# Value sums behind a group's first stage: order of work on PE in a hybrid decoder step

## What is computed

```python
q = (x @ w_query).reshape(t, PEER_HEADS, 2, PEER_DK // 2)
s = jnp.einsum('thcd,ckd->thck', q, sub_keys)
sv, si = lax.top_k(s, PEER_TOPK)
cand = sv[:, :, 0, :, None] + sv[:, :, 1, None, :]      # 16 x 16 sums, top 16 again
top_s, pos = lax.top_k(cand, PEER_TOPK)
g = jax.nn.softmax(top_s, axis=-1)
u = expert_u[experts]
v = expert_v[experts]
a = jax.nn.gelu(jnp.einsum('td,thkd->thk', x, u))
return jnp.einsum('thk,thkd->td', g * a, v)
```

## Time and profile before

| | |
|---|---|
| median of 3 runs | 3510.18 us (3496.6 to 3515.45) |
| profiled execution | 3510.76 us, span 3509.0 us |
| PE busy | 2510.7 us, 72% |
| VectorE busy | 2278.5 us, 65% |
| GpSimd busy | 2300.2 us, 66% |
| ScalarE busy | 813.6 us, 23% |
| value sums on PE (L924) | 4096 matmuls, 1176.0 us |
| u and v gathers | 2048, 1082.26 MB by the software queue |
| all DMA | 1279.45 MB, mean 365 GB/s |
| mean granted clock of PE | 0.839 of full speed |

### The profile page before, as it was taken

How to read it: one execution, slowest core, us unless ns; L and a number is a source line. 1 busy time by engine, 2 the same in 40 slices (tenths; PEclk the granted TensorE clock), 3 DMA queues, 4 the chain that set the end, 5 groups by cost and what they waited for, 6 DMA issues and landing times.

```text
span 3509.0 us, 38717 instructions
## 1 busy us (share of the span) xinstructions
PE 2510.7 (72%) x11488; PEld 1386.8 (40%) x11488; DVE 2278.5 (65%) x5454; ACT 813.6 (23%) x2057; POOL 2300.2 (66%) x2068
## 2 busy tenths in 40 slices
PE   7558775878764598877644977778546888875755
PEld 6426443545531264445311643345213534332421
DVE  3685586655688756657898466558796454544874
ACT  2112212232212212322112123322113122222111
POOL 0466575755657777676777767667777585657774
PEclk9779887999986799898876999889777798988776
DMA  6699899988999999999999999899999999999997
GB/s 237 241 389 375 329 410 333 392 306 302 372 346 373 373 402 372 353 369 412 408 359 375 405 385 355 329 376 409 400 368 374 379 388 359 371 334 398 411 409 305
DMA packets 368935, 1279.45 MB, mean 365 GB/s; under 512 B 59372, under 2 KB 77974, under 8 KB 353368
## 3 DMA queue, kind: packets, MB, share of 16 engines
q0 software_dynamic: 297216, 1082.26, 80.6%
q1 hardware_dynamic: 62324, 168.67, 12.5%
q10 hardware_dynamic: 9188, 26.05, 2.3%
HBM read 1262.31 MB, written 13.48 MB: 364 GB/s over the span
## 4 chain that ended last, share of the span: by engine, by line
DVE 37%; PE 31%; DMA 15%; issue 7%; ACT 4%; SPq 3%; POOL 2%; DVEq 0%; ACTq 0%; POOLq 0%
DVE u_ring L1736 15%; PE acc L924 9%; DMA u_ring<-in_expert_u,pick_cur 8%; PE front L586 8%; PE front L802 3%; DMA v_ring<-in_expert_v,pick_cur 3%; DVE si_u L1603 2%; SPq L536 2%; DVE sv L1602 2%; PE front L711 2%; DMA w_ukT<-in_cache_krope 2%; DVE work L1603 2%; DVE work L1602 1%; DVE work L1647 1%; DVE work L1649 1%
## 5 line engine op out<-in xcount | busy, mean ns | idle before, releaser
L924 PE MATMUL acc<-v_ring,diag 128*64 128x512 f32 x4096 | 1176.0, 723 | 614.6 <-ACT diag L1222 344.4
L1851 POOL DMA_INDIRECT v_ring<-in_expert_v,pick_cur x1024 | 1146.5, 1120 | 607.3 <-PE acc L924 334.3
L1851 POOL DMA_INDIRECT u_ring<-in_expert_u,pick_cur x1024 | 1136.9, 1110 | 569.1 <-issue 292.3
L1736 DVE CUSTOM_DVE_ANT_0 u_ring<-u_ring,xn_cur 128x1024 f32<-128x1024 f32 x1024 | 1209.9, 1222 | 335.1 <-DMA u_ring<-in_expert_u,pick_cur 329.4
L924 PEld LDWEIGHTS acc<-v_ring,diag 128*64 128x64 f32 x4096 | 342.6, 164 | 1331.4 <-issue 878.5
L1222 ACT ACTIVATE diag<-ident,wgt 128x64 f32<-128x64 f32 x1024 | 272.8, 338 | 787.1 <-DVE wgt L1742 734.9
L586 PE MATMUL front<-work,w_ring 128*128 128x256 f32 (+2 forms) x1536 | 306.4, 341 | 31.8 <-DVE mo L1337 17.1
L586 PE MATMUL front<-mo,w_ring 128*128 128x256 f32 (+2 forms) x1536 | 298.2, 335 | 0.0
L1215 ACT ACTIVATE gelu<-dots 128x4 f32<-128x4 f32 x256 | 52.7, 206 | 996.5 <-DVE dots L1736 992.8
L586 PEld LDWEIGHTS front<-work,w_ring 128*128 128x128 f32 x1536 | 249.0, 199 | 83.9 <-issue 28.6
L586 PEld LDWEIGHTS front<-mo,w_ring 128*128 128x128 f32 x1536 | 252.0, 198 | 23.9
(11 more groups left out here) (303 smaller groups left out, 2375.7 us busy)
## 6 DMA issues: line engine op xcount, KB each, us to landing
w_ring<-in_w_pieces SPq DMA_DIRECT2D x112, 1024.0 KB, 8.4
u_ring<-in_expert_u,pick_cur POOLq DMA_INDIRECT x1024, 10.5
v_ring<-in_expert_v,pick_cur POOLq DMA_INDIRECT x1024, 9.9
x_t<-in_x_prompt SPq DMA_DIRECT2D x16, 512.0 KB
v_ring<-in_w_pieces SPq DMA_DIRECT2D x8, 1024.0 KB, 12.0
work<-in_cache_ckv SPq DMA_DIRECT2D x64, 128.0 KB, 15.2
xn_cur<-scratch ACTq DMA_DIRECT2D x14, 512.0 KB, 9.7
scratch_x<-rows_next ACTq DMA_DIRECT2D x8, 512.0 KB, 6.8
```

The lines of the kernel that those rows point to most:

```text
L924: last = nc.tensor.matmul(acc[rows, half, :], diag[:, s % RING, :], v_ring[:, s % RING, half * 512:half * 512 + 512], start=(s < 2), stop= ...
L1736: v.tensor_tensor_reduce(u_ring[:, slot, :], u_ring[:, slot, :], xn2_cur[:, block_of(r), :], 1.0, 0.0, ALU.mult, ALU.add, dots[:, g * G + ...
L1851: pool.indirect_dma_start(ring[:, slot, :], None, a[table][0], bass.IndirectOffsetOnAxis(ap=pick, axis=0)).then_inc(loaded[slot], 16)
```

## The change

PE does the value sums of a group behind its first stage in all groups, not only in those with pages. Which stages a group has, and the order on all other engines, stay.

```diff
@@ -985,11 +985,10 @@
             def tile(it):
 
                 for g, stages in enumerate(PLAN[it]):
-                    ahead = 1 if has_pages(stages) else len(stages)
-                    for s in stages[:ahead]:
+                    for s in stages[:1]:
                         stage(*s)
                     v_group(it, g)
-                    for s in stages[ahead:]:
+                    for s in stages[1:]:
                         stage(*s)
 
             def turn_weights():
```

## The result

The changed kernel takes 3538.84 us (median of 6 runs, 3536.64 to 3541.12) beside 3504.52 us for the kernel before (6 runs): ratio 1.0092, 95% interval 1.0077 to 1.0107. It is slower by 27 to 38 us. The forecast was 3511 us; the time lies in the range, and it is the slower rival's (3547 us) that it is near to. It lies outside the 3493 to 3528 us that the prediction gave its own case.

A forecast was written before the change was run, and what follows sets the result against it. The prediction took tile 1 as paced by the PE, ScalarE, VectorE ping-pong, and GpSimd and DMA as bounding where VectorE awaits u gathers. Costs 41.6 - 16 - 25 = +0.6 us on 3510.76 gave 3511 us; range 3470 to 3550.

The forecast's parts named there:

- the slower rival: Value sums stand ahead of work VectorE needs, full price, no gain from GpSimd: +37 us, 3547 us; chance 0.28.
- The bound of tile 1: From 584 to 912 us the ping-pong of PE, ScalarE and VectorE sets the pace; GpSimd is ahead of need.
- Heads, 8 x 2.55 = 20.4 us: In eight head groups, value sums before the next transpose delay it by 2.55 us each: a cost of 20.4 us.
- Output projection: Value sums ahead of the projection's last piece, which VectorE awaits: 3.6 us in tile 1, 5 at the sample.
- Attention output to mix norm, 5 x 1.7: In five groups, value sums between attention output and the norm's matmul end 1.7 us late: cost 8.6 us.
- the 5.6 us of the query projections: Value sums outlast the 1.16 us gap ahead of the scores: 0.7 us charged in each of eight groups.
- the 5.0 of the query pairs: Two pairs of query stages, charged 2.5 us each for value sums moved between their stages.
- Input projections in tile 4, 2.6 us: Value sums wait for late v gathers, so the projection starts late: net cost 2.6 us.
- Hand-overs, 16 us: At five hand-overs, value sums no longer precede the next group's first stage: gain of 2.5 to 3.6 us each.
- GpSimd's earlier release, 25 us: Earlier value sums let GpSimd issue later gathers sooner, cutting VectorE's u waits: 25 us gained, 0.7 of 35.
- Value sums wait longer for their gathers: PE's wait for v gathers, 269.9 us before, should rise; no size given.
- No effect: DMA is the bound, so costs and gains both vanish: 3511 us; chance 0.16.

The follow-up runs named there:

- Tile 1 alone: Kernel before with value sums moved behind the first stage only in the second tile's groups (19 of the 67): 3644.65 us, ratio 1.0089.
- heads-alone kernel: Kernel before with value sums moved only in the 8 groups that begin with a head and have more than one stage: 3635.77 us, ratio 1.0077.
- the kernel with the value sums inside the stage: Kernel before with value sums put behind the scores, ahead of the value matmuls, in 26 groups whose last stage is a head: 3620.59 us, 1.0015.
- The kernel with the hand-overs alone: Kernel before with value sums moved only in the 15 groups whose first stage is a norm or turn of rows: 3615.75 us, ratio 1.0001.
- All but the heads: Kernel before with value sums moved behind the first stage in all groups but those that hold a head: 3612.13 us, ratio 1.0000.
- the late release: Changed kernel where a v gather also waits until PE has issued the last stage of two groups before: 3669.27 us, 1.0067 against the kernel before.
- the second set: Later runs on the chip numbered 5, with the changed kernel again against the kernel before: 3657.48 us, ratio 1.0039.

## Why the prediction was right or wrong

That 3538.84 us lies between 3470 and 3550 is no merit of the sum. The range took in both rivals; the forecast, no change to speak of, missed by 28 us and had its sign from two sides that cancel, and the prediction gave "slower by over 0.5%" 0.31. What follows takes its terms one by one.

**The bound of tile 1: right.** The prediction had the ping-pong of PE, ScalarE and VectorE set the pace there and GpSimd ahead of need. In the stretch of tile 1 both GpSimd's wait for PE (68.9 to 46.7 us) and VectorE's for u gathers (18.4 to 4.9) got shorter, and it took 19 us longer. Tile 1 alone makes the kernel 0.89% slower.

**Heads, 8 x 2.55 = 20.4 us: right in mechanism, and near in size with some luck.** The transpose of the pattern came 2.5 us behind the scaled probabilities (737.01 to 739.49), as drawn. The eight groups 15, 16, 40, 41, 44, 45, 46 and 88 changed by +0.2, +4.3, +2.4, +3.9, -4.9, +3.4, +3.8 and +2.3 us: 15.4 together, 20.3 without group 44. The single values don't carry the term evenly: groups 16 and 46 have an attention output and no transpose behind the value sums, which the prediction read as the same case; in 44 the transposes became ready only when the value sums were done; 88 is anywhere from 17.4 to 28.8 us in kernels that don't move it; and about 3.6 us of the growth in tile 1 is PE's lower clock, on which the prediction put no price. The heads-alone kernel puts the eight at 28 us (17 to 39 by its interval). The prediction named PE's delay as the price; the place where it counts is VectorE's copy, as the kernel with the value sums inside the stage showed.

**Output projection: right in tile 1, not seen at the sample.** Group 50 grew from 35.28 to 38.82 us, 3.5 where 3.6 was charged. The 5 us of the sample tokens' end aren't there: groups 229 to 235 take 84.5 us before and 84.1 after.

**Attention output to mix norm, 5 x 1.7: not seen.** Group 42 got 1.5 us shorter. The value sums at 761.98 end where the norm's matmul starts (765.56), but VectorE's squares ended at 764.50, so about 1 us is late and the next weight isn't. With all such moves and no heads the time stays at 1.0000, so none of these smaller terms can be told from zero, nor can the 5.6 us of the query projections and the 5.0 of the query pairs.

**Input projections in tile 4, 2.6 us: not seen.** Groups 132 to 136 take 61.5 us before and 60.9 after. The 4.5 us lost in this tile's first part come in group 142 (22.38 to 26.62), where the prediction had nothing; why there, the runs don't tell.

**Hand-overs, 16 us: seen in single places, not in the sum.** The query piece follows the row transposes directly, and starts 0.13 us behind the group's weight where it was 3.39 us: these are the 3.3 us predicted. (The prediction's last paragraph names value sums straight behind the row transposes as the sign; that is the order of before, its own reckoning puts them ahead.)

```profile
916.93 1.97 PE L593 MATMUL front<-ident,rows_next 128*128 128x128 f32 x8 [5.57 <-DVE rows_next L1587]
920.27 3.78 PE L586 MATMUL front<-work,w_ring 128*128 128x256 f32 x8 [1.38 <-DVE mo L1594]
```

Yet group 52 grew from 20.33 to 21.73 us. The eight matmuls of 920.27 take 3.78 us where those of 905.65 took 1.99, at a granted clock of 0.50 for 1.00: before, the value sums ran between PE's idle time and them. And the group's own value sums, 3.65 us, now stand ahead of its key scores. Group 44 did win 4.9 us: its first scores no longer stand behind the value sums of group 43. The largest hand-over was one that the prediction didn't price, and it shows how such a gain is lost. Group 31, before:

```profile
602.58 1.89 PE L586 MATMUL front<-mo,w_ring 128*128 128x256 f32 x8
604.40 3.65 PE L924 MATMUL acc<-v_ring,diag 128*64 128x512 f32 x16
604.50 28.61 SPq L484 DMA_DIRECT2D w_ring<-in_w_pieces  x4
608.19 1.42 DVE L1749 TENSOR_TENSOR y_t<-acc,y_t 128x512 f32<-128x512 f32 x2 [8.45 <-PE acc L924]
```

and after:

```profile
600.77 4.81 PE L924 MATMUL acc<-v_ring,diag 128*64 128x512 f32 x16
606.66 1.41 DVE L1748 TENSOR_TENSOR y_t<-acc,y_t 128x512 f32<-128x512 f32 x2
612.71 25.17 SPq L484 DMA_DIRECT2D w_ring<-in_w_pieces  x4
632.15 0.96 DVE L1356 TENSOR_TENSOR work<-work 128x768 f32<-128x768 f32 x1 [9.47 <-ACT x_t L1092]
```

VectorE waited 8.45 us before for the finished sums of tile 0; with the value sums ahead of the projection piece this wait is gone, and the group is 8.5 us shorter (22.76 to 14.22). But the piece itself ends late, the weight load that waits for it starts 8.2 us later (604.50 to 612.71), and two groups on VectorE waits 9.47 us for the projection: group 33 grows from 6.88 to 16.69 us. PE ran from 605.51 us to this projection without a gap, so it isn't the load that VectorE waited for: the order on PE only chose who waits. The kernel with the hand-overs alone has the same pair (group 31 14.23 us, group 33 14.76) and a ratio of 1.0001.

**GpSimd's earlier release, 25 us: this step failed.** The prediction took 0.7 of 35 us. All but the heads makes nearly all of these moves; by the prediction's own terms it should have stood near 52.6 - 20.4 - 11 - 16 - 25 = -20 us, a ratio of 0.9945, and it was 1.0000 (from 0.9967). With its costs taken as charged, that speaks against the two gains together; what speaks against this one is the waits, and the late release, in which 25 us should have been lost. The u gathers did come earlier: VectorE's wait of 5.62 us in tile 0 is 2.21 us in its place, and over the span its u waits fell by 22.5 us, inside the 20 to 40 that were named. But this was no time won. GpSimd's wait for dot products rose by 133.4 us as its wait for PE fell by 109.4, which the prediction had written down as the sign that the lead is worthless. Nor was there a gain where it was placed, in us from weight to weight: groups 9 to 20, 181.5 to 190.0 (8 predicted); 193 to 200, at the sample's projections, 111.2 to 112.7 (12.5 predicted). The error was in taking a shorter wait of VectorE for u gathers as time won. The ring holds two groups, and GpSimd can't be further ahead of VectorE than that; it got there sooner and stood there. Whether a smaller part of the 25 us exists stays open: the late release cost 12 us beside the change, with nothing to some 20 us by its noise.

**Value sums wait longer for their gathers: right in sign.** PE's wait rose from 269.9 to 319.6 us, and to landing a v gather now takes a median of 11.8 us after 9.9:

```profile
v_ring<-in_expert_v,pick_cur POOLq DMA_INDIRECT x1024, 11.8
```

The granted clock, on which the prediction put no price, stayed at 0.839 in the mean over the span, while it fell in single places (0.50 at 750 us).

**The rivals.** "No effect" was ruled out by the ratio, and with it DMA as the one bound of the whole: tile 1 moves 336 GB/s and the later slices up to 412. The slower rival said "full price and no gain from GpSimd", 37 us; 28 (between the profiled executions) to 34 us (between the medians) were measured first and 12 (3657.48 less 3645.9) in the second set. Its 37 is near partly by luck: it is 52.6 less 16, while the heads alone cost 28 us, and all the rest, the costs outside the heads, the hand-overs and GpSimd's lead, comes to nothing within 12 us together. The forecast was the other case only because two gains of 41 us together were credited from single places. Stretches without a moved group kept their pace, as they had to: groups 70 to 73 took 44.2 us in both kernels and 181 to 191 took 135.3 and 135.2, which are the two that the prediction named. The limit of about 358 GB/s that the prediction took from the Trainium skill ("DMA: Bandwidth & Descriptors", section "Bandwidth") would have left the change without effect. After as before there are slices at 411 and 412 GB/s, and the measurement decides. The section doesn't disagree as much as the prediction has it: it gives the 358 for two cores that stream at once and up to 425 GB/s for one core alone.

## What to carry to other kernels

When work is moved ahead in an engine's queue, ask which engine reads the result that now stands behind it, and whether that reader has anything else to do: 3.65 us of value sums ahead of a 0.55 us transpose cost VectorE 2.4 to 3.9 us in a group, and behind the same transpose and its scores, ahead of the values, no cost was seen (1.0015, 0.9987 to 1.0043). A producer that is released earlier gains only if its ring isn't full when it gets there; look for the wait that will replace the one removed, and credit nothing until the consumer's own wait is shown to be on the path. Work that filled an engine's idle time may also have kept its clock up: look at the lengths of the same matmuls before and after. Try the few places with a clear price apart from the many without: 8 of 67 groups held the price.

## What the runs showed of the hardware

Halving the columns of the value sums took PE's mean granted clock from 0.826 in the changed kernel of that set to 0.737 and 0.738 in the two halved ones. Their time fell by only 1.0 to 1.5%. Other matmuls got longer: those of the projections on L586 took a mean of 346 ns and take 369 (old order) and 364. So a halved step doesn't leave the other steps as they were, and the two halved kernels are to be compared with each other only.

PE's clock fell in places where it had waited longer. Ahead of the values of group 41 it idled 0.27 us before and 2.44 us after, and the same twelve matmuls took 1.60 us at a granted clock of 1.00 and 2.93 us at 0.50. The mean over the span, 0.839 in both kernels, doesn't show this.

The same pair of kernels differed by 0.92% in one set of runs and by 0.39% in another, in which the kernel before is itself 4% slower (3645.9 against 3504.52 us). Group lengths that VectorE and PE set agree to 0.1 us where the clock does (group 41 of the old order: 9.01, 9.01, 9.01 and 9.06 us); the rest, where gathers set the pace, doesn't (groups 86 to 99 took 191.5 and 190.0 us in the first two kernels and 204 to 234 us in all others). That the loss seen in the end depends on how late the gathers are anyway is a guess that no run here tests.
